# Three more groups of expert matrices loaded whole, and one up matrix no longer consumed by quarters

## The reference

```python
def hierarchical_moe(h, wg_r, bg_r, we_r, be_r, w_gate, w_up, w_down):
    # top-1 of 4 groups, then top-2 of the 8 experts in it; 32 experts, FF 512
    ...
    def expert_block(args):
        xb, e = args
        a = jax.nn.silu(xb @ w_gate[e]) * (xb @ w_up[e])   # 1024 -> 512
        return a @ w_down[e]                               # 512 -> 1024
    ...

for l in range(2):
    x = x + mixer(rms_norm(x, norm_mix[l]))
    x = x + hierarchical_moe(rms_norm(x, norm_ffn[l]), ...)
```

## Time and profile before

| | |
|---|---|
| time, median of 3 runs | 1175.86 us (1175.54 to 1176.22) |
| the profiled execution's own time | 1178.19 us |
| its span, first to last instruction | 1176.4 us |
| mean granted TensorE clock | 0.878 of full speed |
| TensorE matmul busy | 881.2 us (75%) |
| VectorE busy, ScalarE busy | 211.4 us (18%), 143.2 us (12%) |
| moved by DMA | 448.49 MB, mean 381 GB/s over the span |

### The profile page before, as it was taken

The page is one execution under the profiler, slowest core; times in us unless marked ns, Lnnn a source line. Parts: engine busy times, 40 slices in busy tenths (PEclk is TensorE's granted clock), DMA queues, the critical chain, the costliest instruction groups (busy, mean ns, idle before and its releaser), DMA issues.

```text
span 1176.4 us, 11498 instructions
## 1 busy us (share of the span) xinstructions
PE 881.2 (75%) x5116; PEld 397.3 (34%) x5116; DVE 211.4 (18%) x438; ACT 143.2 (12%) x271; POOL 10.2 (1%) x11
## 2 busy tenths in 40 slices
PE   8999999756575747475889999977474747474776
PEld 6555545222222222222236655532131313131312
DVE  3812333010101010000026541410000000000001
ACT  4311311000000000000021431110000000000001
POOL 0000010000000000000000000000000000000000
PEclk9999999887787878777999999997888887877889
DMA  9772499999999999999997328999999999999997
GB/s 358 289 282 91 155 423 430 441 428 428 440 431 433 435 433 431 431 433 416 427 422 300 144 84 334 427 442 428 448 431 426 426 437 433 435 435 431 416 425 292
DMA packets 19635, 448.49 MB, mean 381 GB/s; under 512 B 2432, under 2 KB 2688, under 8 KB 5504
## 3 DMA queue, kind: packets, MB, share of 16 engines
q1 hardware_dynamic: 19584, 447.72, 89.7%
HBM read 446.66 MB, written 1.05 MB: 381 GB/s over the span
## 4 chain that ended last, share of the span: by engine, by line
DMA 56%; PE 41%; SPq 1%; another core or an unknown queue 0%; issue 0%; ACT 0%; DVE 0%; DVEq 0%
DMA places<-in_together 47%; PE psum L614 14%; PE psum L992 11%; DMA places<-in_quarters 8%; PE psum L1094 5%; PE psum L989 4%; PE psum L560 1%; DMA places<-in_w_in 1%; PE psum L1034 1%; PE psum L548 1%; PE psum L541 1%; PE psum L1121 0%; PE psum L536 0%; PE psum L683 0%
## 5 line engine op out<-in xcount | busy, mean ns | idle before, releaser
L614 PE MATMUL psum<-places,mixed 128*32 128x512 f32 x3040 | 421.7, 708 | 280.6 <-DMA places<-in_together 253.6
L614 PEld LDWEIGHTS psum<-places,mixed 128*32 128x32 f32 x3040 | 110.5, 127 | 574.8 <-issue 443.5
L992 PE MATMUL psum<-places 128*128 128x512 f32 x288 | 126.3, 593 | 0.0
L992 PEld LDWEIGHTS psum<-places 128*128 128x128 f32 x288 | 53.6, 190 | 61.4 <-issue 61.2
L560 PEld LDWEIGHTS psum<-sel,h 128*128 128x128 f32 x528 | 60.4, 192 | 17.0 <-issue 15.1
L560 PE MATMUL psum<-sel,h 128*128 128x128 f32 x528 | 64.3, 279 | 1.7 <-DVE sel L779 1.7
L803 DVE TENSOR_TENSOR mixed<-psum,sig 128x512 f32<-128x512 f32 x16 | 16.9, 1058 | 256.4 <-PE psum L614 256.4
L548 PE MATMUL psum<-y_sb,spread 128*128 128x512 f32 x128 | 59.6, 606 | 2.1 <-ACT y_sb L748 1.4
L734 ACT COPY mixed<-psum 128x512 f32<-128x512 f32 x34 | 19.7, 587 | 315.9 <-PE psum L560 315.9
L800 DVE TENSOR_TENSOR sig<-psum,sig 128x512 f32<-128x512 f32 x16 | 11.1, 691 | 241.0 <-ACT sig L739 241.0
L989 PE MATMUL psum<-places 128*128 128x256 f32 x192 | 44.5, 392 | 1.5 <-DMA places<-in_w_in 1.5
(11 more groups left out here) (261 smaller groups left out, 521.6 us busy)
## 6 DMA issues: line engine op xcount, KB each, us to landing
places<-in_quarters SPq DMA_DIRECT2D x22, 2048.0 KB, 35.2
places<-in_w_gate SPq DMA_DIRECT2D x16, 2048.0 KB, 26.1
places<-in_w_in SPq DMA_DIRECT2D x12, 2048.0 KB, 30.8
places<-in_w_down SPq DMA_DIRECT2D x8, 2048.0 KB, 15.6
places<-in_w_up SPq DMA_DIRECT2D x8, 2048.0 KB, 12.4
places<-in_w_out SPq DMA_DIRECT2D x4, 2048.0 KB, 14.0
places<-in_quarters SPq DMA_DIRECT2D x4, 1024.0 KB, 46.4
places<-in_w_in SPq DMA_DIRECT2D x2, 1024.0 KB, 28.1
```

Of the source, the lines that this page charges most:

```text
L614: mm = pe.matmul(psum[slots, out + n, :], inp[:, c, slots], slot(layer, unit)[:, at + 512 * n:at + 512 * (n + 1)], start=c == 0, stop=c == ...
L992: mm = pe.matmul(banks[:, m, :], hT[:, c, m * P:(m + 1) * P], w[:, c, :], start=c == 0, stop=c == KC - 1)
```

## The change

```diff
-QUARTERED = ((0, 0), (QUADS - 1, 1), (QUADS - 1, 2))
-TOGETHER = range(16, 84)
+QUARTERED = ((0, 0), (QUADS - 1, 2))
+TOGETHER = (*range(8, 12), *range(16, 92))
...
                 sp.wait_ge(S["gated"], 2 + layer)
                 if layer == 1:
                     sp.wait_ge(S["mix_turned"], 4)
-                for u in (8, 9, 10, 11, 4, 5):
+                load_matrices(layer, 8)
+                for u in (4, 5):
                     load_expert_unit(layer, u)
```

## The result

The changed kernel takes 1179.85 us (median of 7 runs, 1179.23 to 1183.47), the kernel before 1177.03 us in 7 runs (1175.54 to 1177.91). The ratio is 1.0034, with a 95% interval of 1.0024 to 1.0043: 2.8 to 5.1 us slower. (It is an estimate from all the runs; the quotient of the two medians is 1.0024, at the interval's lower edge.) The forecast was 1180.0 us, +4.1 us (0.35%), and its range, 1178.2 to 1182.0, held.

What follows compares the result with a forecast made beforehand. DMA was taken to bound the MoE, TensorE layer 1's mixer. +2.5 us (layer 0) and +1.6 (layer 1) make +4.1: 1182.3 from the profiled 1178.19, less 2.3 for the runs' median, 1180.0; range 1178.2 to 1182.0.

Steps and rivals of the forecast that it cites:

- H: Start of the matmuls on the last half-quarter of each layer's last down; before, 596.10 in layer 0, 1165.75 in layer 1.
- What it removes: Stream ahead of each layer's last up: 9 transfers fewer per layer, so that up lands 3 × 0.22 = 0.66 us sooner.
- the gain of 0.22 us a matrix: In the DMA stream: a whole matrix takes 19.34 us, four quarters 19.56; 0.07 us for each transfer removed.
- The 2.0 us of the Trainium skill: Fixed cost per DMA; in a row, 18 fewer would give 36 us, about 1145; transfers-cost-more rival, chance 0.03.
- What it adds: Each layer's last up: all 64 matmuls stand behind the landing, 9.2 us (8.5 to 9.9), where 16 took 1.86.
- From the up's end to H: Each layer's end: 3.14 us gathering to copies, three down quarters of 1.86, two sets of six fillers of 1.30.
- The chain overtakes the stream: Each layer's end: TensorE's way from the up's landing takes 20.5 us, transfers need 18.2 or 17.3, so it sets H.
- The parts costed at nothing: Quad 0's down and quad 7's gate whole, 18 fewer SP issues, and layer 1's later mixer weights: no cost.
- The mixer weights of layer 1: Layer 1's first weights issue at 587.3 instead of 574.01, covered by 10 us of stream; dry-stream rival 2 us more, chance 0.08.
- The sum: Both layers: +2.5 us in layer 0, passed on by the mixer, and +1.6 in layer 1, +4.1 us; chance 0.70.

Runs made afterwards that it cites:

- the two that should show it alone: Against the kernel before: quad 0's down and quad 7's gate whole, 1.0001; the changed kernel with fillers ahead of the last up, none in the last down, 0.9991.
- The run with the last up by quarters: Kernel before with quad 0's down and quad 7's gate whole, the last up still by quarters: 1176.53 against 1176.59 us, ratio 1.0001.

## Why the prediction was right

| from the up's last landing to H, us | layer 0 | layer 1 |
|---|---|---|
| before | 17.31 | 18.24 |
| predicted for the change | 20.5 | 20.5 |
| after | 20.61 | 19.99 |
| only the last up whole | 20.10 | 21.35 |
| last up by units | 20.82 | 19.94 |
| last up whole in layer 0 only | 21.30 | 18.02 |
| last up whole in layer 1 only | 17.20 | 21.18 |
| change without fillers in the last down | 18.19 | 17.03 |
| change with fillers ahead of the up | 18.66 | 18.93 |
| change with twice the fillers in the last down | 22.89 | 22.85 |
| before with twice the fillers | 17.19 | 18.17 |

(By the starts of the matmuls that waited for the landing, and of the line of `last_half`, L683 to L686.)

**What it removes.** In its own place, from the wait on quad 7's gate to the one on its up, the whole matrix took 19.28 and 19.33 us; before, the quarters took 20.04 in layer 0 and 19.56 in layer 1. The prediction's 19.34 for a whole matrix was read from the fastest three in a row: over the long streams of both traces whole matrices come 19.46 us apart on average, since now and then one takes 19.8 to 20.4. Set against that average the gain of 0.22 us a matrix would be 0.1, so its size is not settled. By the chain the change gave −0.75 us on the way to layer 1's last up, where 0.66 was said, but only −0.11 in layer 0, where, it seems, landings that wander by up to 1 us lay in the way. No run shows the gain in the time beyond its interval; the two that should show it alone stand at 1.0001 and 0.9991. The 2.0 us of the Trainium skill that the prediction set beside it are there a fit to transfers issued by GpSimd ("DMA: Bandwidth & Descriptors", section "Anatomy of one DMA — SWDGE (gpsimd) path"), while SP issues these; here 18 transfers fewer gave nothing near 36 us.

**What it adds.** The up took 8.95 us in layer 0 (575.55 to 584.50) and 8.33 in layer 1, where 9.2 was taken and 8.5 given as the lower bound: 0.2 and 0.9 less. Over the ten last ups that come whole and without fillers ahead of them in the traces here, it is 8.33 to 9.68 us, in the mean 8.9, so the term was 0.3 us too long. That the length is the clock's was argued from the other quads and is now shown, by 7.00 us with the fillers ahead of it. Single us of the changed kernel's up in layer 0, behind 7.23 us of idle, have a granted clock of 0.50 at its start and of 1.00 later on:

```profile
575.55:576.55 1.00, 1.00 (x8) 0.34 (x12) 0.00 (x0) 0.00 (x0) 0.00 (x0) 0.50 1.11 475
...
579.55:580.55 1.00, 1.00 (x16) 0.25 (x12) 0.00 (x0) 0.00 (x0) 0.00 (x0) 1.00 0.96 410
```

The rule of the Trainium skill ("TensorE: Matmul & The Clock Gate", section "HAM oscillation — how this bites in real kernels") that was weighed there, that a burst behind such a wait starts at half clock, holds here.

**From the up's end to H.** 3.2 us for the gathering and transposes (3.14 predicted), and the down with its fillers took 8.43 (1158.38 to 1166.81), where 3 × 1.86 + 2 × 1.30 = 8.18 was worked out: six fillers between matmuls of the other kind took 1.49, not 1.30. This and the shorter up went against each other.

**The chain overtakes the stream.** Shown twice over: H has no DMA wait, and fillers cost their full length after and nothing that can be measured before.

**The parts costed at nothing.** Quad 0's down and quad 7's gate: nothing measurable in the run that has them alone. The mixer weights of layer 1 were issued at 584.59 in place of 574.01, or 13.7 us later with the 3.13 us of the start taken out, where some 13 were said. That is 13.2 us ahead of 597.8, until when the prediction had the stream busy:

```profile
584.59 0.81 SPq L448 DMA_DIRECT2D places<-in_w_in  x2
```

It cost nothing. The DMA share is 0.97 or more in every stretch of 3 to 5 us from 585 to 620, before and after, and from H of layer 0 through layer 1's mixer and routing both kernels take the same time: in the chain, the 112 matmuls that end quad 0's gate and up in layer 1 start 157.53 us behind H before (753.63 − 596.10) and 157.51 after (753.67 − 596.16). This fits a mixer that takes its length from H on, whenever H is.

**The sum.** +2.5 and +1.6 were predicted. The two traces give +3.2 (3.30 − 0.11) in layer 0 and +1.0 (1.75 − 0.75) in layer 1: the sum came out as closely as it did partly because one layer's miss made up for the other's. The runs with one layer alone, for which these terms gave +2.1 and +1.2 us, measured +1.5 and +1.1 us, with 1 us to either side. The whole measured +4.0 by the ratio. The level, 1180.0 against 1179.85, fits better than it had a right to: the kernel before itself was 1.2 us above its first three runs when it was timed again, and the difference of the two medians is 2.8 us.

## What to carry to other kernels

Merging the last transfers ahead of an end trades a small gain (an estimate of 0.07 us for each removed, from the spacing of the landings) against all the work that could have been done on the earlier pieces; near the end of a stream compare the work left behind the last landing with what the transfers behind it leave free, and merge only while it fits. Fillers that keep the clock up are free only as long as the engine waits behind them anyway: when a change takes that wait away, they become the first thing to remove. A test with the suspected work doubled, on both kernels, tells cheaply who owns the path.

## What was not expected of the hardware

- A whole matrix of 8 MB counts as many DMA packets as a unit of 2 MB: 19635 packets became 17043, 2592 fewer, which is 144 for each of the 18 transfers removed. It fits all transfers of the queue, from 1 KB to 8 MB: its 136 issues count 19584 packets before, its 118 issues 16992 after, 144 for each.
- SP's issues of the last halves went faster. The two of layer 1, before, then after:

```profile
1119.30 7.98 SPq L384 DMA_DIRECT2D places<-in_quarters  x2
```

```profile
1118.43 0.91 SPq L384 DMA_DIRECT2D places<-in_quarters  x2
```

  They took 7.98 us and 0.91 us (in layer 0, 9.63 and 0.91). Fewer transfers were queued ahead of them after the change; that this is the reason is not tested. They landed some 46 us behind their issue in both kernels, so nothing waited for the issuing.
- A stretch of 16 matmuls in the last down is not at the full clock in the run with only layer 0 changed, behind 2.36 us of idle and in spite of the fillers; these and the last half's 8 behind them took 2.46 and 1.93 us in place of 1.92 and 1.06, at a granted clock of 0.75 and 0.50:

```profile
1163.79 2.46 PE L616 MATMUL psum<-places,mixed 128*32 128x512 f32 x16 [2.36 <-DMA places<-in_quarters]
1166.24 1.93 PE L685 MATMUL psum<-places,mixed 128*32 128x512 f32 x8
```

  The run with the last up by quarters shows the same behind 2.91 us of idle: 2.37 us at 1157.21 (clock 0.79), and the six fillers behind it took 2.76 us in place of 1.56 (0.54). In the kernel before, the 16 matmuls behind 2.63 us of idle kept the full clock (1.00).
- The link of 64 matmuls of the first projection took 15.77 us in two of the twelve profiled executions and 14.08 in the other ten, and transfers of the same bytes wandered by about 1 us. What moves these landings stays open; it is why gains under 1 us are not settled here.
